# Mixer heads: tiles weighed in the turn of their argument, the pair's second head sum behind the weights' products

## The chip, the cores and the metric

The kernel runs on one core of one Trainium2 chip. The metric is the device time of one execution in microseconds (us). Engines are named as in the profile: PE (TensorE matmul), PEld (its weight loads), DVE (VectorE), ACT (ScalarE), POOL (GpSimd), SP (SyncE, which issues the DMAs).

## What is computed

The reference is two transformer blocks over 512 tokens of width 1024. The stage that matters here is in the first block's token mixer. It holds the four heads of an mLSTM (`M_HEADS` 4, head width 128), and beside them the preparation of eight RWKV-7 heads, in four pairs. The reference writes the mLSTM in chunks; what it computes per head is

```python
d = jnp.where(causal, b[..., :, None] - b[..., None, :] + logi[..., None, :], -jnp.inf)
p = jnp.exp(d - m_t[..., None]) * jnp.einsum('bhctd,bhcsd->bhcts', q, k)
num = ... + jnp.einsum('bhcts,bhcsv->bhctv', p, v)
den = ... + jnp.sum(p, -1)
h = num / jnp.maximum(jnp.abs(den), jnp.exp(-m_t))[..., None]
hm = standardize_heads(h, NORM_EPS)
y_m = jax.nn.sigmoid(o) * hm * m_norm_g
```

and, for the RWKV heads, what a pair's preparation makes of the projected rows:

```python
w = jnp.exp(-DECAY_SCALE * jax.nn.sigmoid(r_w0 + jnp.tanh(wd) @ r_w_up))
a = jax.nn.sigmoid(r_a0 + ad @ r_a_up)
kk = kk / jnp.maximum(jnp.sqrt(jnp.sum(kk * kk, -1, keepdims=True)), 1e-12)
kr = kr * (1.0 + (a - 1.0) * r_ka)
yr = yr + jnp.sum(rr * kr * r_rk, -1, keepdims=True) * vr
```

## The kernel before

All engines run programs of their own, tied by semaphores. Work is in stages; the change is in one of them, in the function `mlstm` (L1348). It computes a head over the whole sequence at once: for head h and block j of 128 keys, the scores against the queries from block j on, a tile of 128 keys by 512, 384, 256 or 128 queries. That makes sixteen **turns**, n = 4h + j, in a loop that each engine has in its own program. The order of the work in a turn is written out by hand.

What belongs to tile n, and the lines that show in the profile:

- DVE, `argument` (L1527): the exponent's argument from the row `top_b` and a column, two instructions, L1536 and L1537, into one of four buffers `m_e`. The buffer must be free of tile n-4.
- ACT: the exponent, L1685; right behind it the cast of a streamed weight tile to its high half (L388), on which POOL's subtraction for the low half depends (L397, `split_low`). I call POOL's part the split.
- PE: the scores, L1580, which wait until the tile before the last is weighed (the score banks are two).
- DVE, `weigh` (L1517): L1523 multiplies the scores in PSUM into the tile, L1525 multiplies its first 128 columns with the causal mask; both operands of L1525 are in SBUF. I call it the masking multiply.
- PE, `nums` (L1410): the weights' products, L1418 with the values and L1419 with ones, summed over the head's four tiles.

Beside them, in each turn:

- PE emits 4 + 4 steps of **fill**: the projection of another 128 columns of the first block, three fp32r products of 128x512 a step (L436, L437, L438). DVE (or ACT, for the four jobs "o") takes the finished job out of PSUM in the next turn; on DVE that is `shifted`, L1810 and L1812.
- The head before is normed: PE sums (`norm_sums`, L1474 in step j = 1, L1478 in j = 2), ACT (`norm_functions`, L1486, L1487, L1490, L1493), DVE (`norm_values`: L1499 centring in j = 1, L1504 and L1506 in j = 2, the reciprocal L1510 in j = 3) and `norm_end` (L1513, L1515) at the start of the next head.
- A pair of RWKV heads is prepared (`Operands`, L1816), step (n-1) % 4 in turn n, from turn 1 on. Step 0 (j = 1): PE's gate products, L1837 and at the end of the turn L1853; ACT's sigmoids L1860 and L1864; DVE L1889 to L1899. Step 1 (j = 2): PE's first head sum L1842, ACT's root L1870 and exponents, DVE L1903 and the reciprocal L1904. Step 2 (j = 3): DVE L1906, L1907 and the bonus terms L1909. Step 3 (j = 0 of the next head): PE's second head sum L1846, a product of `ones_half` with the bonus terms; DVE L1914, L1915, L1916 and, with that sum, L1921, which says that the pair's operands are made; POOL L1930 and L1932. L1837 of the next pair waits for L1921.
- Two rows per head are spread over the partitions by PE (`spread_top` at the end of turn 4h+3, `spread_low` at j = 0, both L1429, four rows of weights) and copied by ACT (L1460, L1467).

Before the change DVE weighs tile n-1 at the start of turn n, ahead of the argument of tile n:

```python
            for n in range(MH * ST):
                h, j = divmod(n, ST)
                if n:
                    weigh(dve, chain, n - 1)
                argument(dve, chain, n)
```

On PE the scores, the low row's spread and, in turns 4, 8 and 12, the second head sum stand ahead of the fill and the weights' products of tile n-1. Behind the loop comes the rest of the stage: the last head's norm, the last pair's step 3, the last fill job, and the recurrence's first group (L2006, L2021, L2163 and on), which goes on over the same engines.

Of the kernel before, what the change touches and what calls it, by code (L numbers as in the profile page):

```python
# [30 lines left out]
ST = S // P  # L31
# [6 lines left out]
MW, MH, MHD = 512, 4, 128  # L38
# [1309 lines left out]
def mlstm(k, h_in, arriving, early, qk, v, o, rkv, wa, gd, lora, lora_g, pairs, rooms, core, raw, norm):  # L1348
# [51 lines left out]
    fill = Fill(k, jobs, arriving, early=early)  # L1400
    GATES_JOB, WA, VALUES, UNITS = (2 * MH + i for i in range(4))
    arrived = lambda pair, part: fill.taken(names.index(f"{part}{pair.p}"))
# [3 lines left out]
    def prep(n):  # L1406

        return [(pairs[(n - 1) // ST], (n - 1) % ST)] if 0 < n <= MH * ST else []
# [35 lines left out]
    def spread_low(pe, h):  # L1444
        if h == 0:

            pe.wait_ge(*G("floor_ready").ge(2))
        if h < MH - 1:
            pe.wait_ge(*G("spread_taken").ge(top_nth(h + 1)))
        else:  # L1450

            pe.wait_ge(*G("var_ready").ge(h))
        spread(pe, low, h)
# [85 lines left out]
    with k.stage() as block:  # L1539
# [15 lines left out]
        @block.tensor  # L1555
        def _(pe):
            fill.pe(pe, 2 * DT + DT // 2)
            arriving.pe_sums(pe)
            fill.pe(pe, DT // 2)
            arriving.pe_turns(pe)  # L1560
            fill.pe(pe, (2 * MH + 2 + ST) * DT - 3 * DT)

            pe.wait_ge(*G("rows_ready").ge(1))
            for t in range(ST):
                last = nc.tensor.matmul(k.banks[SPREAD][:, t * MH:(t + 1) * MH], u[:, t * P:(t + 1) * P],
                                        k.const("ident", MH)[:, 0:MH], start=True, stop=True)
            last.then_inc(*G("turned_ready").inc())
            spread_top(pe, 0)
            fill.pe(pe, 4)

            pe.wait_ge(*fill.taken(VALUES))
            pe.wait_ge(*G("silu_ready").ge(2 * MH))
            pe.wait_ge(*k.tables_landed)
            pe.wait_ge(*k.lora_landed)
            for n in range(MH * ST):
                h, j = divmod(n, ST)
                if n >= 2:

                    pe.wait_ge(*prob.ge(n - 1))
                nc.tensor.matmul(k.banks[SCORE[n % 2]][:, 0:width[j]], qk[h][:, 1, j * P:(j + 1) * P],  # L1580
                                 qk[h][:, 0, j * P:S], start=True, stop=True).then_inc(*sent.inc())
                if h and j == 0:
                    spread_low(pe, h - 1)
                for pair, step in prep(n):
                    if step == 3:
                        pair.pe(pe, 2)
                fill.pe(pe, 4)
                if n:
                    nums(pe, n - 1)
                if h:  # L1590
                    norm_sums(pe, h - 1, j)
                for pair, step in prep(n):
                    if step < 2:
                        pair.pe(pe, step)
                if n:
                    fill.pe(pe, 4)
                for pair, step in prep(n):
                    pair.pe_late(pe, step)
                if j == ST - 1 and h + 1 < MH:
                    spread_top(pe, h + 1)  # L1600

            fill.pe(pe, 4)
            nums(pe, MH * ST - 1)
            fill.pe(pe, 4)
            spread_low(pe, MH - 1)

            pe.wait_ge(*G("operands_made").ge(2))
            pe.wait_ge(*G("values_made").ge(4))
            core.pe_turn(pe, 0, 0, range(2))
            pe.wait_ge(*fill.taken(LAST - 1))  # L1610
            core.pe_turn(pe, 0, 0, range(2, 3))

            pe.wait_ge(*G("den_ready").ge(MH))
            core.pe_turn(pe, 0, 0, range(3, 4))
            norm_sums(pe, MH - 1, 1)
            last_pair.pe(pe, 2)

            pe.wait_ge(*fill.taken(LAST))
            core.pe_products(pe, 0, 0)
            norm_sums(pe, MH - 1, 2)  # L1620
            core.pe_z(pe, 0, 0)

            core.pe_lane_free(pe, 0)
            pe.wait_ge(*G("var_ready").ge(MH))
            pe.wait_ge(*G("operands_made").ge(PAIRS))
            pe.wait_ge(*G("values_made").ge(2 * PAIRS))
            core.pe_turn(pe, 0, 1, range(4))
            core.pe_products(pe, 0, 1)
            core.pe_gate(pe, 0)
            core.pe_z(pe, 0, 1)  # L1630
            core.pe_gate(pe, 1)
            core.pe_rest(pe, 0)
            core.pe_group(pe, 1)
# [86 lines left out]
        @block.vector  # L1720
        def _(dve):
            chain = Chain(dve, G("dve_step"))
            nc.vector.memset(hm[:, 0:1], 0.0).then_inc(*G("gains_ready").inc())
            early.dve(dve, 0, 4)
            k.split_first(dve)
            early.dve(dve, 4, DT)
            arriving.dve_adds(dve, 0, 4)
            arriving.dve_adds(dve, 4)
            arriving.dve_roots(dve)

            dve.wait_ge(*arriving.named("turned_ready").ge(1))
            nc.vector.tensor_copy(hm[:], k.banks[arriving.turn_bank]).then_inc(*G("high_made").inc())
            arriving.dve_parts(dve, 0, DT)
            c = VECTORS["mu_rkv"]
            chain(nc.vector.tensor_scalar(k.keep_share[:], k.vecs[:, c:c + 15], -1.0, 1.0, ALU.mult, ALU.add))
            for t in range(2 * MH):
                fill.take(dve, chain, t)
            fill.take(dve, chain, GATES_JOB)
            dve.wait_ge(*G("gate_taken").ge(1))
            nc.vector.scalar_tensor_tensor(out=tmp, in0=fpre, scalar=-1.0, in1=fpre, op0=ALU.mult,  # L1740
                                           op1=ALU.max).then_inc(*G("abs_ready").inc())
            fill.take(dve, chain, WA)

            dve.wait_ge(*G("ln_ready").ge(1))
            chain(nc.vector.scalar_tensor_tensor(out=fpre, in0=fpre, scalar=0.0, in1=tmp, op0=ALU.min, op1=ALU.subtract))
            chain(nc.vector.tensor_tensor_scan(run, fpre, fpre, 0.0, ALU.add, ALU.bypass))
            nc.vector.tensor_tensor(u, ipre, run, ALU.subtract).then_inc(*G("rows_ready").inc())
            dve.wait_ge(*G("rows_ready").ge(1))
            chain(nc.vector.tensor_tensor_scan(top, u, u, 0.0, ALU.max, ALU.max))
            nc.vector.tensor_tensor(low, top, run, ALU.add).then_inc(*G("rows_ready").inc())  # L1750

            dve.wait_ge(*G("floor_ready").ge(1))
            chain(nc.vector.tensor_scalar(low, low, EPS, 1e-37, ALU.mult, ALU.max))
            nc.vector.tensor_scalar(low, low, 1e37, None, ALU.min).then_inc(*G("floor_ready").inc())

            dve.wait_ge(*G("turned_ready").ge(1))
            nc.vector.tensor_copy(u_col[:].rearrange("p t h -> p (t h)"), k.banks[SPREAD][:, 0:ST * MH]).then_inc(*G("turned_taken").inc())
            dve.wait_ge(*G("turned_taken").ge(1))
            dve.wait_ge(*k.tables_landed)
            for n in range(MH * ST):  # L1760
                h, j = divmod(n, ST)
                if n:
                    weigh(dve, chain, n - 1)
                argument(dve, chain, n)
                if h >= 2 and j == 0:
                    norm_end(dve, chain, h - 2)
                if n and jobs[UNITS + n - 1].engine == "dve":
                    fill.take(dve, chain, UNITS + n - 1)
                if n == MH * ST - 1:
                    weigh(dve, chain, n)  # L1770
                if h:
                    norm_values(dve, chain, h - 1, j)
                if n == MH * ST - 1:
                    norm_end(dve, chain, h - 1)
                for pair, step in prep(n):
                    pair.dve(dve, step, arrived)
            fill.take(dve, chain, LAST)
            norm_values(dve, chain, MH - 1, 1)
            last_pair.dve(dve, 3, arrived)
            core.dve_masks(dve, 0, 0, 0)  # L1780
            norm_values(dve, chain, MH - 1, 2)
            core.dve_masks(dve, 0, 0, 1)
            core.dve_masks(dve, 0, 0, 2)
            norm_values(dve, chain, MH - 1, 3)
            norm_end(dve, chain, MH - 1)
            for step in range(3):
                core.dve_masks(dve, 0, 1, step)
            core.dve_rest(dve, 0)
            core.dve_group(dve, 1)
# [2625 lines left out]
```

## Time and profile before

| | us |
|---|---|
| median of 3 runs | 1657.27 |
| lowest, highest | 1655.9, 1658.98 |
| profiled execution, its own time | 1661.74 |
| its span, first to last instruction | 1660.0 |
| PE busy in the span | 1594.6 (96%) |
| DVE busy in the span | 913.0 (55%) |
| mean granted clock of PE | 0.995 |

Times in rows of a timeline are us from the start of the span. The ends of products on PE are modelled, so starts are the better measure there. In windows the columns are the busy us (with the number of instructions) of PE, PEld, DVE, ACT and POOL, then the granted PE clock as a share of 2.4 GHz, the DMA share and GB/s. The stage's loop lasts from about 98 to 256 us.

### The profile page before, as it was taken

Reading aid. Unit: us, or ns where it says so; the run is one execution under the profiler, and the core shown is the slowest. Engines: PE = TensorE matmul, PEld = TensorE weight load, DVE = VectorE, ACT = ScalarE, POOL = GpSimd, SP = SyncE. Lnnn points to the kernel's source line nnn. Section 1 sums busy time; section 2 is a strip of 40 time slices with the busy share of each in tenths; the row PEclk is TensorE's granted clock in tenths of the full one; section 3 lists DMA queues with packets and bytes.
Section 4 is the critical chain, followed back from the end, with each engine's and each line's share of the span. In section 5 each row is a group of like instructions: output and inputs, shape, how many; then the busy total and the mean of one; then the engine's idle time right before and its main releaser. Section 6 shows DMA issues by size and latency. Waiting matters only on the chain. (4 is left out here: it accounts for less than half of the span.)

```text
span 1660.0 us, 25020 instructions
## 1 busy us (share of the span) xinstructions
PE 1594.6 (96%) x10298; PEld 1228.3 (74%) x10298; DVE 913.0 (55%) x1464; ACT 689.9 (42%) x1184; POOL 712.8 (43%) x357
## 2 busy tenths in 40 slices
PE   6999998889999899999999999999999999999999
PEld 5876666778787588888888888566576577787787
DVE  5957878545852336565541148597736663324251
ACT  4544444333432443222232334433645456355441
POOL 4533336244653144555554446264133422463342
PEclk9999999999999999999999999999999999999999
DMA  5421111003432032333233333112112310442132
GB/s 183 136 78 62 51 51 53 4 29 91 152 115 76 14 102 77 100 102 101 91 103 95 105 116 124 34 64 77 39 45 68 99 61 29 140 157 84 52 100 78
DMA packets 39713, 138.54 MB, mean 83 GB/s; under 512 B 4400, under 2 KB 5680, under 8 KB 38320
## 3 DMA queue, kind: packets, MB, share of 16 engines
q1 hardware_dynamic: 39600, 136.94, 25.8%
q8 instruction: 82, 1.34, 0.3%
q14 instruction: 31, 0.25, 0.0%
HBM read 132.73 MB, written 4.19 MB: 82 GB/s over the span
## 5 line engine op out<-in xcount | busy, mean ns | idle before, releaser
L397 POOL TENSOR_TENSOR parts<-ring,parts 128x1024 fp32r<-128x1024 f32 (+3 forms) x250 | 582.1, 2335 | 800.4 <-ACT parts L388 800.2
L436 PE MATMUL banks<-h_hi,parts 128*128 128x512 f32 x1120 | 462.6, 413 | 3.4 <-PEq L296 3.4
L438 PE MATMUL banks<-h_hi,parts 128*128 128x512 f32 x1120 | 437.3, 390 | 0.0
L437 PE MATMUL banks<-h_lo,parts 128*128 128x512 f32 x1120 | 436.9, 390 | 0.0
L388 ACT CAST parts<-ring 128x1024 fp32r<-128x1024 f32 (+3 forms) x251 | 244.7, 978 | 134.7 <-PE banks L438 134.6
L436 PEld LDWEIGHTS banks<-h_hi,parts 128*128 128x128 f32 x1120 | 211.0, 188 | 63.1 <-issue 19.6
L437 PEld LDWEIGHTS banks<-h_lo,parts 128*128 128x128 f32 x1120 | 211.0, 188 | 46.7 <-issue 6.1
L438 PEld LDWEIGHTS banks<-h_hi,parts 128*128 128x128 f32 x1120 | 210.5, 188 | 45.0
L3131 ACT CAST ffn_act_hi<-ffn_gate 128x512 fp32r<-128x512 f32 x22 | 13.7, 622 | 162.9 <-DVE ffn_gate L3030 162.9
L436 PE MATMUL banks<-ffn_act_hi,parts 128*128 128x512 f32 x176 | 68.5, 389 | 0.0
L437 PE MATMUL banks<-ffn_act_lo,parts 128*128 128x512 f32 x176 | 68.5, 389 | 0.0
L438 PE MATMUL banks<-ffn_act_hi,parts 128*128 128x512 f32 x176 | 68.5, 389 | 0.0
L3087 DVE TENSOR_TENSOR ffn_raw<-banks,ffn_root 128x512 f32<-128x512 f32 x22 | 15.2, 691 | 87.2 <-PE banks L438 87.1
L3097 DVE TENSOR_TENSOR x<-x,banks 128x512 f32<-128x512 f32 x8 | 5.5, 687 | 88.3 <-PE banks L438 88.3
L1075 DVE SCALAR_TENSOR_TENSOR ffn_gate<-ffn_raw,vecs,ffn_gate 128x511 f32<-128x511 f32 (+1 forms) x44 | 50.4, 1145 | 1.6
L2754 ACT ACTIVATE scores<-scores,row_stats 128x128 f32<-128x128 f32 (+3 forms) x64 | 35.5, 556 | 29.9 <-DVE row_stats L2732 29.8
L1071 DVE TENSOR_SCALAR ffn_gate<-ffn_raw,vecs 128x512 f32<-128x512 f32 x22 | 42.3, 1924 | 0.8
L436 PEld LDWEIGHTS banks<-ffn_act_hi,parts 128*128 128x128 f32 x176 | 33.0, 188 | 6.9
L437 PEld LDWEIGHTS banks<-ffn_act_lo,parts 128*128 128x128 f32 x176 | 33.0, 188 | 6.9
L438 PEld LDWEIGHTS banks<-ffn_act_hi,parts 128*128 128x128 f32 x176 | 33.0, 188 | 6.7
L2742 DVE TENSOR_SCALAR scores<-scores,row_stats 128x128 f32<-128x128 f32 (+3 forms) x64 | 34.6, 541 | 2.3
L2794 ACT ACTIVATE h_hi<-x,vecs 128x512 fp32r<-128x512 f32 x16 | 11.6, 726 | 50.9 <-DVE x L3076 27.1
(607 smaller groups left out, 2978.5 us busy)
## 6 DMA issues: line engine op xcount, KB each, us to landing
ring<-weights SPq DMA_DIRECT2D x211, 512.0 KB, 3.5
ring<-weights SPq DMA_DIRECT2D x24, 256.0 KB, 2.6
x<-xT SPq DMA_DIRECT2D x4, 1024.0 KB, 6.0
ring<-weights SPq DMA_DIRECT2D x8, 384.0 KB, 3.1
x_spill<-x SPq DMA_DIRECT2D x2, 1024.0 KB, 4.8
x<-x_spill SPq DMA_DIRECT2D x1, 2048.0 KB, 9.3
outT<-x SPq DMA_DIRECT2D x8, 256.0 KB, 2.0
ring<-weights SPq DMA_DIRECT2D x8, 192.0 KB, 2.4
```

The costliest lines, as they stand in the source:

```text
L388: self.nc.scalar.copy(self.parts[:, t % PARTS, 0, 0:w], self.ring[:, t % SLOTS, 0:w]).then_inc(self.high_ready, 1)
L397: self.nc.gpsimd.tensor_tensor(self.parts[:, t % PARTS, 1, 0:w], self.ring[:, t % SLOTS, 0:w], self.parts[:, t % PARTS, 0, 0:w].bitcast(F3 ...
L436: nc.tensor.matmul(out, w.hi, x.hi, start=first, stop=False)
L437: nc.tensor.matmul(out, w.hi, x.lo, start=False, stop=False)
L438: return nc.tensor.matmul(out, w.lo, x.hi, start=False, stop=last)
L1071: chain(nc.vector.tensor_scalar(dst, bank, k.vec(f"{weights}{taps - 1}", tile), k.vec(bias, tile), ALU.mult, ALU.add))
L1075: ins = nc.vector.scalar_tensor_tensor(out=dst[:, lag:S], in0=bank[:, 0:S - lag], scalar=k.vec(f"{weights}{j}", tile), in1=dst[:, lag:S], ...
L2742: nc.vector.tensor_scalar(scores(j - 1, e), scores(j - 1, e), st[:, 3:4], None, ALU.mult).then_inc(*scaled.inc())
L2754: nc.scalar.activation(scores(j, e), scores(j, e), ACT.Exp, bias=small[:, u % NS, 1:2], scale=-1.0, accum_out=small[:, u % NS, 2:3]).then_ ...
L2794: nc.scalar.mul(self.h.hi[:, m, :], k.x[:, m, :], k.vec(self.gain, m)).then_inc(*G("h_high").inc())
L3087: nc.vector.tensor_tensor(r, bank(gate_job(f)), root, ALU.mult).then_inc(*G("gate_taken").inc())
L3131: nc.scalar.copy(act_t.hi[:, f, :], gate[:, f % GATES, :]).then_inc(*G("act_high").inc())
```

## The change

In PE's turn, the fill's first four steps and the weights' products of tile n-1 now stand ahead of the second head sum (step 3 of a pair, turns 4, 8 and 12). In DVE's turn, tile n is weighed in turn n itself, behind its argument, the end of the norm two heads before and the take of a fill job; tile n-1 is no longer weighed at the start. In turns with j = 3, the pair's step (with the bonus terms) stands ahead of the norm's reciprocal; in the other turns the norm values come first, as before.

```diff
@@ PE, turn n
                 if h and j == 0:
                     spread_low(pe, h - 1)
+                fill.pe(pe, 4)
+                if n:
+                    nums(pe, n - 1)
                 for pair, step in prep(n):
                     if step == 3:
                         pair.pe(pe, 2)
-                fill.pe(pe, 4)
-                if n:
-                    nums(pe, n - 1)
                 if h:
                     norm_sums(pe, h - 1, j)
@@ DVE, turn n
                 h, j = divmod(n, ST)
-                if n:
-                    weigh(dve, chain, n - 1)
                 argument(dve, chain, n)
                 if h >= 2 and j == 0:
                     norm_end(dve, chain, h - 2)
                 if n and jobs[UNITS + n - 1].engine == "dve":
                     fill.take(dve, chain, UNITS + n - 1)
-                if n == MH * ST - 1:
-                    weigh(dve, chain, n)
-                if h:
+                weigh(dve, chain, n)
+                if h and j < ST - 1:
+                    norm_values(dve, chain, h - 1, j)
+                for pair, step in prep(n):
+                    pair.dve(dve, step, arrived)
+                if h and j == ST - 1:
                     norm_values(dve, chain, h - 1, j)
                 if n == MH * ST - 1:
                     norm_end(dve, chain, h - 1)
-                for pair, step in prep(n):
-                    pair.dve(dve, step, arrived)
             fill.take(dve, chain, LAST)
```

## Rows read from the trace of the kernel before

**Rows 1.** The page, part 1: busy us, share of the span, instructions

```profile
PE 1594.6 (96%) x10298; PEld 1228.3 (74%) x10298; DVE 913.0 (55%) x1464; ACT 689.9 (42%) x1184; POOL 712.8 (43%) x357
```

**Rows 2.** Windows of ten us: busy us by engine, granted clock, DMA

```profile
198.00:208.00 10.00, 9.63 (x40) 7.07 (x39) 8.61 (x12) 6.90 (x10) 3.36 (x2) 1.00 0.16 54
208.00:218.00 10.00, 9.65 (x27) 5.17 (x26) 9.76 (x13) 2.73 (x4) 3.77 (x2) 0.83 0.16 52
```

**Rows 3.** Waits in the stage, 90 to 270 us: total us, times, longest

```profile
DVE m_hm L1499 <- PE banks L1474: 14.5, 4, 6.0
...
PE banks L1418 <- DVE m_e L1525: 3.4, 8, 0.8
```

**Rows 4.** Timeline of PE, turns 2, 3: start us, us, what, [idle before]

```profile
117.43 0.39 PE L437 MATMUL banks<-h_lo,parts 128*128 128x512 f32 x1
117.66 0.39 PE L438 MATMUL banks<-h_hi,parts 128*128 128x512 f32 x1
118.41 0.91 PE L1418 MATMUL banks<-m_e,m_v 128*128 128x384 f32 x2 [0.37 <-DVE m_e L1525]
...
127.36 0.70 PE L1418 MATMUL banks<-m_e,m_v 128*128 128x256 f32 x2 [0.82 <-DVE m_e L1525]
```

**Rows 5.** Timeline of PE, turns 4, 8, 12: the head sum and its surroundings

```profile
134.40 2.07 PE L1846 MATMUL banks<-x,consts 128*128 128x512 f32 x2
...
139.65 0.38 PE L1418 MATMUL banks<-m_e,m_v 128*128 128x128 f32 x2
...
174.54 1.12 PE L1846 MATMUL banks<-x,consts 128*128 128x512 f32 x2 [0.38 <-DVE x L1909]
...
178.25 0.38 PE L1418 MATMUL banks<-m_e,m_v 128*128 128x128 f32 x2
...
213.12 2.08 PE L1846 MATMUL banks<-x,consts 128*128 128x512 f32 x2 [0.35 <-DVE x L1909]
...
218.31 0.38 PE L1418 MATMUL banks<-m_e,m_v 128*128 128x128 f32 x2
```

**Rows 6.** Timeline of POOL: two of the splits of weights

```profile
102.06 2.44 POOL L397 TENSOR_TENSOR parts<-ring,parts 128x1024 fp32r<-128x1024 f32 x1 [6.95 <-ACT parts L388]
...
198.37 2.85 POOL L397 TENSOR_TENSOR parts<-ring,parts 128x1024 fp32r<-128x1024 f32 x1 [9.66 <-ACT parts L388]
```

**Rows 7.** Tile m_e: the masking multiply, ns min/median/max

```profile
L1525 DVE TENSOR_TENSOR m_e<-m_e,consts x16: 291/291/2274, 102.6 to 247.9; 128x128 f32<-128x128 f32 x16
```

**Rows 8.** Timeline of DVE: turns 0, 10 to 13, the stage end

```profile
102.61 2.04 DVE L1525 TENSOR_TENSOR m_e<-m_e,consts 128x128 f32<-128x128 f32 x1
...
195.43 0.56 DVE L1523 SCALAR_TENSOR_TENSOR m_e<-banks,m_e 128x384 f32<-128x384 f32 x1
...
196.23 0.35 DVE L1536 TENSOR_SCALAR m_e<-top_b,u_col 128x256 f32<-128x256 f32 x1
...
198.27 0.68 DVE L1504 TENSOR_TENSOR y<-y,floor_b 128x512 f32<-128x512 f32 x1
...
204.92 0.42 DVE L1523 SCALAR_TENSOR_TENSOR m_e<-banks,m_e 128x256 f32<-128x256 f32 x1
...
217.21 1.38 DVE L1914 COPY decay<-x 128x8 f32<-128x8 f32 x1
...
219.10 1.78 DVE L1916 TENSOR_TENSOR rkv<-x,rkv 128x512 f32<-128x512 f32 x1
220.92 0.69 DVE L1921 TENSOR_TENSOR rkv<-banks,rkv 128x512 f32<-128x512 f32 x1
...
259.86 0.69 DVE L1499 SCALAR_TENSOR_TENSOR m_hm<-banks,m_hm 128x512 f32<-128x512 f32 x1 [1.25 <-PE banks L1474]
```

**Rows 9.** Timeline of PE: the gate products of a pair

```profile
187.50 1.12 PE L1837 MATMUL banks<-wa,lora_wa 64*128 64x512 f32 x2
...
191.50 1.12 PE L1853 MATMUL banks<-wa,lora_wa 64*128 64x512 f32 x2
...
231.56 1.12 PE L1853 MATMUL banks<-wa,lora_wa 64*128 64x512 f32 x2
```

## The prediction

> **What bounds the kernel now.** I read the page first: PE is busy for 96% of the span [rows 1], so only what makes PE wait or slows it is worth time. The change touches one stage, the sixteen turns from about 98 to 256 us. Its windows of ten us show PE busy for 9.6 us or more of each ten, DVE for up to 9.8 [rows 2]. So the gain can only be the rest of PE's time and its clock, and DVE is the engine that could take PE's place. I then took the waits of the stage, and the timelines of PE, DVE, ACT and POOL through it.
>
> PE loses time in three ways. First, the weights' products (L1418) wait for DVE's masking multiply (L1525): eight times, 3.4 us by the column of idle time [rows 3]. The starts tell more, since idle time is counted from a modelled end. A fill product starts 0.23 us after the one before; the first of these waits starts 0.75 us after, so 0.52 us are lost; the one with 0.82 us of idle time lost 0.97 [rows 4]. The other six (turns 6, 7, 10, 11, 14, 15) look like the first. They are alike because DVE is itself tied to PE: it masks the tile as the last thing after work that waited for PE's gate product or head sum.
>
> Second, the pair's second head sum (L1846) waits for DVE's bonus terms (L1909) in turns 8 and 12, 0.38 and 0.35 us [rows 5]; turn 4 shows none.
>
> Third, the clock. From the start of L1846 to the weights' products of the same turn stands the same work each time: 3.71 us in turn 8, but 5.25 in turn 4 and 5.19 in turn 12 [rows 5]. The window of turn 12 has a granted clock of 0.83 [rows 2], a mean over 2.4 GHz and a stretch at 1.2. Ahead of each such place PE runs four full-width f32 products in a row with L1846 the last, two of them with four rows of weights. The falls cost 1.48 and 1.54 us.
>
> **The change part by part.** No instruction is added or removed, no DMA moves, SP and POOL keep their orders; what changes is PE's order within a turn and DVE's.
>
> Weighing in the turn of the argument: DVE now weighs tile n a turn sooner, ahead of the norm values and the pair's step. PE wants tile n only in the middle of its turn n+1. In turn 10 the tile would be ready some 5 us after DVE's argument, and PE asks for it a turn later. All eight waits go: 7 x 0.52 + 0.97 = 4.6 us. The price on DVE is a wait for ACT's exponent and PE's score. Where a fill tile is taken between the two (1.5 us), the exponent is done before. Where ACT takes the fill (turns 5, 9, 13), DVE waits some 0.6 us for it; queued behind is the centring L1499, which waits for PE anyway, 14.5 us in four times [rows 3]. So nothing.
>
> The head sum behind the products, its terms ahead of the reciprocal: the terms no longer stand behind DVE's reciprocal of the head, and they are wanted 3.3 us later (twelve fill products of 0.23 and two narrow pairs). The 0.38 and 0.35 go, with their ends some 0.8 us. On DVE the bonus product L1921 waits for this sum, and the next turn's argument is queued behind it. In turn 12 PE would end the sum at 213.12 + 3.3 + 0.9, less what it gained, so before 217.3, while DVE stands at L1921 at 220.92 [rows 5, 8]. Nothing.
>
> The clock: between the spread of the row and the head sum now stand twelve fill products, so the row of f32 products ends a quarter sooner. Both falls go, 3.0 us; the other end is that neither goes. I take that they go: turn 8 shows that even the long row of f32 products does not always lower the clock, and the window of turn 10, with pairs of them between fills, is at 1.00 [rows 2].
>
> Sum of what PE gains: 4.6 + 0.8 + 3.0 = 8.4 us.
>
> Against it stands a price on DVE. POOL splits a weight tile each turn, started by ACT's cast, which follows ACT's exponent: 2.44 us long when alone [rows 6]. The masking multiply takes 0.29 us, but 2.04 us in turn 0, where it begins within such a split and ends with it; before, this was seldom, the median being 0.29 [rows 6 to 8]. In the new order it is the rule. In turn 10 the argument starts at 196.23, the split at 198.37, 2.14 later; the take ends at 198.27, and behind a weighing of 0.42 the masking multiply would start 2.5 us after the argument and stand until the split ends at 4.6 [rows 6, 8]. That is 2.1 us of delay in turns of this kind, and as much in turns 11 and 14; in turn 12, 0.5. The Trainium skill (SBUF — State Buffer, Who interferes with whom) says that a DVE instruction with two SBUF inputs and a POOL instruction exclude each other and the first holds the port to its end; by that rule, too, DVE pays here and POOL does not, and the trace agrees in turn 0.
>
> What it costs PE is read on the loop from one pair's second gate product (L1853) to the next pair's, since DVE hangs on the first and PE's L1837 on DVE's L1921. PE's own loop is 231.56 - 191.50 = 40.06, less 0.52, 0.52, 0.4 and the fall of 1.48: 37.1 us [rows 9]. DVE's: L1921 ends at 221.61, 30.1 after L1853; add two delays of 2.1; in turn 12 the waits of 1.2 and 1.1 that L1914 and L1916 have behind POOL now (1.38 and 1.78 us for some 0.2 and 0.7 of work [rows 8]) give way to 0.5 and about 1.2, so less 0.6; and 4.0 from L1837 to L1853 [rows 9]: 37.7. PE waits 0.6 us at L1837 in turns 9 and 13: 1.2 us. The bounds: 0 if the splits miss, 1.8 each if POOL goes ahead at each meeting.
>
> At the end of the stage DVE is late by the delay of turn 14 (2.1) and does not share PE's last two gains (1.05), but has the 0.8 us of one weighing moved out of its way and 1.25 us of slack ahead of L1499 [rows 8]: 1.1, call it 1.0 us late. The recurrence behind it hangs on DVE, so this counts. Turns 2 and 3, with the same collisions, come ahead of the first head's norm work, where DVE has time to spare; nothing.
>
> 8.4 - 1.2 - 1.0 = 6.2 us. The stages behind are chains relative to this one, and weights are far ahead there, so I take the shift to reach the end. The span goes from 1660.0 to 1653.8. The profiled execution took 1661.74, so 1655.5 in its like. It is 4.5 us over the median, so the runs may have fewer falls of the clock; I leave the sum as it is: 1657.27 - 6.2 = 1651.1.
>
> **Rivals.** (A) The forecast, gain 3.8 (PE waits 1.8 us at L1837 in both turns, for 0.6) to 7.4 (no wait there), so 1649.9 to 1653.5.
>
> (B) The collisions cost PE nothing: split and multiply miss each other, or slack covers it. Gain 8.4, 1648.9 us. For it: in turn 10 the multiply would begin only 0.4 us after the split. Against: turn 11's narrow tile is weighed well inside the split.
>
> (C) The falls of the clock stay, as the three f32 products ahead remain: 8.4 - 3.0 - 2.2 = 3.2 us gained, 1654.1. For it: in turn 4 the clock fell with PE never idle, and in turn 8 it held in the same order, so the row alone does not decide. The Trainium skill (TensorE: Matmul & The Clock Gate, What's actually happening) has the clock go down after idleness and stay up under work; by that rule the order of products would change nothing, as in this rival; turn 4 speaks against the rule.
>
> (D) Slower: DVE becomes the bound. Place: DVE from the argument of turn 10 to L1921 in turn 12, and its like one head before. If POOL's products each go ahead (1.2 and 1.1) and each split is itself stretched to the 2.85 us of [rows 6], the loop is 37.7 + 2.3 + 0.8 = 40.8, and PE waits 3.7 at L1837 twice; with 1.4 at the end and a fall of 1.5 behind each wait: 8.4 - 7.4 - 1.4 - 3.0 = -3.4, 1660.7 us. It decides from a loop over 39.3 us, the mean of the two as they are.
>
> (E) It does not do what it says for the end: PE's time is won in the stage and lost behind it, in the recurrence or by other falls of the clock. Within 0.2%, near 1656.
>
> **How the numbers follow.** A 0.50, B 0.15, C 0.19, D 0.06, E 0.10. Likeliest is A, 1651.1. The range takes A, B but for its edge, and C with some of E: 1648.3 to 1655.5. A measurement of this kernel can tell about 0.2%, 3.3 us, from no change. C lies on that line and goes half and half: faster 0.75, same 0.19, slower 0.06.
>
> **What would show it.** In the changed profile: L1418 waits for L1525 nowhere, L1846 for L1909 nowhere; the time from the head sum on shows no clock of 0.83; the median of L1525 goes from 0.29 to near 2 us (B: it does not); PE waits at L1837 in turns 9 and 13 for L1921, 0 to 1.8 us; L1499 of the stage's end starts 6 us sooner. I am wrong if the stage ends sooner but the kernel does not, if the masking multiply stays short, or if the clock falls in the same places.

## The result, and the profile after

The changed kernel is slower: 1663.72 us, the median of 22 runs (1660.04 to 1667.86), against 1658.98 for before in 21 runs beside it. The ratio is 1.0026, with a 95% interval of 1.0017 to 1.0035. Medians, means and ratios here and below leave out four executions of over 2000 us: one of before beside this kernel, one of before and two of e8 later. I had forecast 1651.1 with a range up to 1655.5, and 0.06 for a slower kernel. The profiled execution took 1660.88 us, among the shortest of its kind, where that of before (1661.74) was among the longer ones; so the two spans, 1659.1 and 1660.0, stand the wrong way round, and I compare them place by place.

The waits of PE in the stage (98 to 262 us) of the changed kernel: total us, times, longest.

```profile
PE banks L2005 <- ACT y L1487: 3.9, 1, 3.9
PE banks L436 <- DVE rkv L1811: 3.4, 3, 1.6
```

The same view of before: 

```profile
PE banks L1418 <- DVE m_e L1525: 3.4, 8, 0.8
PE banks L1846 <- DVE x L1909: 0.7, 2, 0.4
PE banks L2006 <- ACT y L1487: 0.2, 1, 0.2
```

The waits that were to go have gone, all ten. In their place PE's fill (L436) waits three times for DVE's take of a fill tile, and the first product of the recurrence (L2005, the L2006 of before) waits 3.9 us for ACT in place of 0.2. Rows name lines by their own kernel's numbers, which differ by up to three from those of before behind the changed part: the terms L1906 to L1909 of before are L1905 to L1908 here.

The masking multiply (tile m_e, L1525, ns min/median/max) is long nearly always, as forecast; before, the median was 291 [rows 7]:

```profile
L1525 DVE TENSOR_TENSOR m_e<-m_e,consts x16: 291/2197/2250, 101.1 to 243.0; 128x128 f32<-128x128 f32 x16
```

The windows of ten us (columns as in [rows 2]) show the head sum's window at clock 1.00, where it was 0.83 [rows 2], but PE busy for 8.41 us in place of 9.65; and the stage's end, where before had 10.00 busy in 248 to 258 us:

```profile
208.00:218.00 10.00, 8.41 (x36) 6.20 (x35) 9.82 (x11) 2.55 (x4) 3.61 (x2) 1.00 0.10 34
248.00:258.00 10.00, 6.05 (x26) 3.36 (x25) 8.12 (x8) 2.64 (x5) 1.37 (x2) 0.92 0.17 53
258.00:268.00 10.00, 7.26 (x201) 5.17 (x200) 8.57 (x15) 6.41 (x9) 7.51 (x5) 0.84 0.32 109
```

Measured by the starts of PE's scores (L1580), the lead over before grows from 1.5 us at the loop's start (a fall of the clock near 24 us, in the profile of before alone) to 7.1 us in turn 15: 5.6 us won in the loop, the two falls of the clock among them. From one turn's scores to the next, a turn that had one of the waits for L1525 is 0.63 to 0.64 us shorter now, turn 3 with the long one 1.08; the turns 9 and 13, in which the fill waits for the take, are 1.31 and 1.83 longer. At PE's last spread (L1429) the lead is 6.6 us, at the last group of the recurrence's first products (L2006, here L2005) 2.9, and at L1499 2.5 (257.39 against 259.86 [rows 8]). The place where it goes is seen in DVE's timeline of turn 15:

```profile
242.97 2.25 DVE L1525 TENSOR_TENSOR m_e<-m_e,consts 128x128 f32<-128x128 f32 x1
245.14 0.68 DVE L1905 TENSOR_TENSOR x<-x 128x512 f32<-128x512 f32 x1
245.85 2.79 DVE L1906 TENSOR_TENSOR qk<-qk,x 128x512 f32<-128x512 f32 x1
248.68 0.75 DVE L1908 SCALAR_TENSOR_TENSOR x<-rkv,vecs,x 128x512 f32<-128x512 f32 x1
249.35 3.35 DVE L1510 RECIPROCAL y<-y 128x512 f32<-128x512 f32 x1
252.73 0.75 DVE L1513 SCALAR_TENSOR_TENSOR m_hm<-m_hm,vecs,y 128x512 f32<-128x512 f32 x1
253.52 0.69 DVE L1515 TENSOR_TENSOR y<-m_hm,m_o 128x512 f32<-128x512 f32 x1
```

The pair's terms (L1905 to L1908) now stand ahead of the reciprocal and the norm's end, and two of the seven instructions run into POOL's splits at 242.65 and 245.50. The first of these, 2.25 us, is not new: the masking multiply of this turn took 2.27 us before too. New are L1906 with 2.79 us and the place of the terms. So L1515 starts only 0.83 us sooner than before, where PE is 6.6 ahead. Before:

```profile
254.35 0.69 DVE L1515 TENSOR_TENSOR y<-m_hm,m_o 128x512 f32<-128x512 f32 x1
```

In the changed kernel L1515 ends at 254.2, and ACT and PE hang on it one behind the other:

```profile
254.30 0.58 ACT L1486 COPY m_hm<-banks 128x512 f32<-128x512 f32 x1 [3.65 <-DVE y L1515]
```

```profile
255.44 0.66 PE L2005 MATMUL banks<-consts,rkv 128*128 128x128 f32 x4 [3.95 <-ACT y L1487]
```

Later a second loss stands in the state steps of the recurrence, at 375 to 385 us, 2.4 us large. The second of PE's steps (L2399, here L2398) starts 4.08 us behind the first, where it was 2.60. The experiments come back to it.

### The profile page after: what moved, and what is told of

It reads as the page before. It is cut to its first block and busy times, and to the rows that moved or that the text cites. A ratio compares the mean times of both kernels' runs of the same rounds, so it can differ in the third digit from the quotient of the medians.

```text
span 1659.1 us, 25026 instructions
## 1 busy us (share of the span) xinstructions
PE 1593.0 (96%) x10298; PEld 1228.8 (74%) x10298; DVE 930.3 (56%) x1464; ACT 689.8 (42%) x1184; POOL 707.5 (43%) x357
## 5 line engine op out<-in xcount | busy, mean ns | idle before, releaser
L436 PE MATMUL banks<-h_hi,parts 128*128 128x512 f32 x1120 | 461.4, 412 | 6.8 <-DVE rkv L1811 3.4
L436 PEld LDWEIGHTS banks<-h_hi,parts 128*128 128x128 f32 x1120 | 210.5, 188 | 69.3 <-issue 21.3
L436 PE MATMUL banks<-ffn_act_hi,parts 128*128 128x512 f32 x176 | 68.5, 389 | 0.0
L436 PEld LDWEIGHTS banks<-ffn_act_hi,parts 128*128 128x128 f32 x176 | 33.0, 188 | 6.9
```

What stands on the lines that cost most here:

```text
L436: nc.tensor.matmul(out, w.hi, x.hi, start=first, stop=False)
```

## The experiments

Times scatter mainly with the clock: over all runs of the study 0.001 less mean granted clock goes with 1.3 us. Beside each median and ratio I therefore give the difference of the means at an equal clock of 0.995, by that slope; its standard error is 0.3 to 0.5 us. Where an edit itself makes PE idle and its clock fall, as in e2, this difference leaves part of the loss out. The experiments were timed in three groups, each with before again: 1659.55 us in 29 runs for e1 to e4, 1660.90 in 34 for e5 to e8, 1658.65 in 29 for e9 to e11; ratios and differences are against the group's own. The clocks of before's runs beside the changed kernel are not on record, so its difference is taken against the first group's: +4.0 us (+3.5 against the second's, +5.1 against the third's). Where an experiment is compared with the changed kernel, that spread stands behind it.

In the experiments D names the theory that the loss sits on DVE (not the prediction's rival D), P that PE's new order costs, L that the last turn alone does it; F, that the place of DVE's instructions in its stream matters.

**PE's move alone** (e1_pe_only): DVE as before.

```
                 fill.pe(pe, 4)
                 if n:
                     nums(pe, n - 1)
+                for pair, step in prep(n):
+                    if step == 3:
+                        pair.pe(pe, 2)
```

> Only PE's part of the change: the second head sum (L1846) stands behind the fill's first four steps and the weights' products; DVE is as before. Theory D (the loss sits on DVE: the masking multiply stands behind POOL's split, DVE is late at the stage's end, PE waits for ACT's L1486 and its clock falls): 0 to 2 us faster than before (the L1846 waits of 0.8 us go, and the falls of the clock in turns 4, 8 and 12 where a run has them). Theory P (PE's new order costs): 2 to 4 us slower. In the profile by both: L1525 keeps a median of 0.29 us and L1418 waits for it eight times.

1658.02 us in 11 runs against 1659.55 for before in 29; ratio 0.9986 (0.9973 to 0.9998); at equal clock -1.35, as D had it. P is out. The waits for L1909 are gone, the eight for L1525 are there as before:

```profile
PE banks L1418 <- DVE m_e L1525: 3.3, 8, 0.8
```

**DVE's weighing alone** (e2_weigh_only): `weigh(dve, chain, n)` behind the take, with the second head sum and the pair's step where they were.

> Only the weighing in the turn of the argument; PE's order and the place of the pair's step behind the norm values are as before. Theory D: the masking multiply has a median of 2.2 us, and the stage's end is late by the collisions of turns 14 and 15: 1 to 3 us slower than before. Theory L (what costs is the last turn alone, the end of the norm of head 2 behind the pair's step, on which ACT's L1486 waits): 2 to 5 us faster than before, since the last turn keeps its order here. PE waits for L1846's terms up to 2 us in turns 8 and 12 by both.

1669.9 us in 6 runs, ratio 1.0062 (1.0048 to 1.0076); at equal clock +5.5. PE's head sum, still ahead of the fill, now waits for bonus terms that stand behind the weighing and the reciprocal:

```profile
PE banks L1843 <- DVE x L1906: 9.9, 2, 5.0
```

Both theories expected waits of up to 2 us there, and the run is 10 us slower by the medians, beyond D's 3: the clock, 0.9917 in the mean against 0.9951, fell behind the waits. The weighing needs one of the other two parts, and L as the only cause is out.

**The mask on the scores** (e3_mask_in_psum): the changed kernel, the mask multiplied into the scores in PSUM, ahead of the weighing.

```
+        chain(nc.vector.tensor_tensor(score[:, 0:P], score[:, 0:P], k.const("key_le_query"), ALU.mult))
         nc.vector.scalar_tensor_tensor(out=ed, in0=score[:, 0:width[j]], ...
-        nc.vector.tensor_tensor(e[:, n % 4, 0:P], e[:, n % 4, 0:P], k.const("key_le_query"), ALU.mult)
```

> The changed kernel with the mask multiplied into the scores in PSUM, ahead of the weighing, so that the masking multiply has one operand in SBUF instead of two; same count of instructions. Theory D: the multiply is short (about 0.3 us) though POOL's split runs beside it, the wait of PE for ACT's L1487 at the stage's end shrinks from 4 us to under 2, and the kernel is 3 to 6 us faster than the changed one, about as fast as before or 1 to 2 us faster. Theory L: the multiply is short, but PE still waits 2 us or more at the end: at most 2 us faster than the changed kernel. Theory P: no more than 1 us off the changed kernel.

1664.11 us in 12 runs, ratio 1.0024 (1.0015 to 1.0034); at equal clock +2.4. By the ratio that is no faster than the changed kernel, against D's expectation of 3 to 6 us and within L's; at equal clock 1.6 us may be won, the fill's waits for the take are 2.1 us in place of 3.4, and the state steps lose less in this profile (below). The bulk stays, 3.7 us of waiting at the stage's end among it: the masking multiply is short now, but the next instruction with two inputs in SBUF has its wait. DVE in turn 15 of this kernel:

```profile
242.59 0.29 DVE L1524 TENSOR_TENSOR banks<-banks,consts 128x128 f32<-128x128 f32 x1
242.92 0.29 DVE L1525 SCALAR_TENSOR_TENSOR m_e<-banks,m_e 128x128 f32<-128x128 f32 x1
243.13 2.43 DVE L1906 TENSOR_TENSOR x<-x 128x512 f32<-128x512 f32 x1
245.59 2.81 DVE L1907 TENSOR_TENSOR qk<-qk,x 128x512 f32<-128x512 f32 x1
```

So the collision belongs to the split's time and not to the masking multiply: whatever of the kind follows the take pays the rest of the split.

**The last turn in before's order** (e4_last_turn): in turn 15 the reciprocal, `norm_values` and `norm_end` stand ahead of the pair's step.

```
-                if h and j < ST - 1:
+                last = n == MH * ST - 1
+                if h and (j < ST - 1 or last):
                     norm_values(dve, chain, h - 1, j)
+                if last:
+                    norm_end(dve, chain, h - 1)
```

> The changed kernel with the order of before in the last turn alone: the reciprocal and the end of the norm of head 2 ahead of the pair's step. Theory D: PE's wait at the stage's end shrinks from 4 us by the pair's step (2.1 us, and 2.1 more where its L1907 stood behind a split), so 2 to 4 us faster than the changed kernel, still no faster than before by more than 1 us. Theory L: 4 us or more faster than the changed kernel, and 1 us or more faster than before. Theory P: within 1 us of the changed kernel.

1660.74 us in 12 runs, ratio 1.0003 (0.999 to 1.0016); at equal clock +0.4, so 3.6 less than the changed kernel, as D had it; L had expected a kernel faster than before. The wait at the stage's end is 0.2 us again, the window of 248 to 258 us has PE busy for 9.17:

```profile
PE banks L436 <- DVE rkv L1812: 3.5, 3, 1.7
PE banks L1478 <- issue: 0.9, 1, 0.9
PE banks L2006 <- ACT y L1487: 0.2, 1, 0.2
```

**The state steps.** In the changed kernel, e2 and e4, all with the new weighing, PE's second state step stands 4.1 us behind the first; before and in e1 it is 2.6. In e3 it is 2.63: there a stretch at half clock (376 to 380 us at 0.57) brought the first step late, and DVE's add met only the end of POOL's split (0.94 us); the fourth step is 1.0 us late. The new order makes the kernel six instructions longer, with DVE's arithmetic the same in number: the pages count 25026 against 25020, and x1464 for DVE in both. I put them down to wait instructions in DVE's stream. To see whether that is all, e5_before_waits takes before and adds only waits that are long satisfied, and e6_last_turn_waits moves the stream of e4 on by two:

```
             dve.wait_ge(*k.tables_landed)
+            for _ in range(13):
+                dve.wait_ge(*k.tables_landed)
             for n in range(MH * ST):
```

> Before, with 13 waits more on DVE ahead of the mlstm loop, on a load that has long landed: six instructions more in DVE's stream, as the changed kernel has, and no other difference. F (the 2.4 us at the state steps come from where DVE's instructions stand: the first add L2405 starts some 0.46 us behind its satisfied wait in place of 0.10, so L2407 loses the port to POOL's split): the second state step starts 4.1 us behind the first in place of 2.6, and the run is slower than before by 1.5 to 2.8 us. W (the loss comes from the weighing's order by some state that it leaves behind, such as POOL's or ACT's lead): the distance stays 2.6 and the time is before's within 0.5 us.

1663.42 us in 12 runs against 1660.90 for before in 34; ratio 1.0017 (1.0003 to 1.0032); at equal clock +2.8. DVE at the first state step, before:

```profile
380.26 0.43 DVE L2405 TENSOR_TENSOR state<-banks,decay 128x256 f32<-128x256 f32 x1 [1.40 <-PE banks L2399]
380.72 0.42 DVE L2407 TENSOR_TENSOR state<-state,gain 128x256 f32<-128x256 f32 x1
```

and with the waits (its lines are higher by one):

```profile
377.63 0.42 DVE L2406 TENSOR_TENSOR state<-banks,decay 128x256 f32<-128x256 f32 x1 [1.76 <-PE banks L2400]
378.09 2.37 DVE L2408 TENSOR_TENSOR state<-state,gain 128x256 f32<-128x256 f32 x1
```

```profile
377.77 4.96 POOL L397 TENSOR_TENSOR parts<-ring,parts 128x1024 fp32r<-128x1024 f32 x2 [16.48 <-ACT parts L388]
```

```profile
380.51 0.68 PE L2400 MATMUL banks<-state,step_T 64*64 64x64 f32 x16 [1.41 <-DVE state L2408]
```

The multiply from the bank starts 0.36 us later behind the same product. The add behind it has two inputs in SBUF; before, it started 0.05 us ahead of POOL's split, at 380.72 against 380.77, and took 0.42; here the split begins at 377.77, 0.32 us ahead of the add, which takes 2.37. The second step starts 1.5 us late by this and the fourth, behind another such meeting, 2.4 (10.2 us behind the first in place of 7.8). F holds, with no other edit in the kernel.

> The last-turn variant (label e4_last_turn) with 5 such waits, two instructions more in DVE's stream, so that the late instruction is another one than L2405. F: the second state step starts 2.6 us behind the first, the run is faster than e4_last_turn by 1.5 to 2.8 us, so about 1658.3, level with before. W: distance 4.1, time as e4_last_turn within 0.5 us.

1658.47 us in 11 runs, ratio 0.998 (0.9969 to 0.9992); at equal clock -1.7. The second step stands 2.59 us behind the first, and against e4 2.1 us are won, as F had it. This version is faster than before and than the changed kernel.

> The changed kernel with 5 redundant waits on DVE ahead of the loop (two instructions more in its stream), and nothing else. F: the second state step starts 2.6 us behind the first in place of 4.1, and of the loss against before 2 to 3 us are gone: ratio 1.0005 to 1.0015. G (e6 gained against e4 by something else, the time of the runs being scattered by the clock): ratio 1.002 or above.

The changed kernel with five such waits: 1660.98 us in 11 runs against 1658.65 for before in 29; ratio 1.0015 (1.0006 to 1.0025); at equal clock +2.5. F's distance is there, its time only at the edge: 1.5 us of the changed kernel's +4.0 are gone, not 2 to 3, and the interval reaches into G. The second step stands 2.6 us behind the first:

```profile
380.30 0.42 DVE L2405 TENSOR_TENSOR state<-banks,decay 128x256 f32<-128x256 f32 x1 [1.41 <-PE banks L2399]
380.76 0.43 DVE L2407 TENSOR_TENSOR state<-state,gain 128x256 f32<-128x256 f32 x1
```

> Before with 17 such waits, eight instructions more in DVE's stream in place of e5_before_waits' six. F (place decides, not number): the second state step starts 2.6 us behind the first, the time is before's within 0.7 us. H (the waits' number costs, each a little, or any shift of the stream from before's does it): distance 4.1, slower than before by 1.5 us or more.

Before with eight instructions more: 1660.25 us in 12 runs, ratio 1.0011 (1.0 to 1.0023); at equal clock +0.5. The distance is 2.59, so the place in the stream and not the number of waits makes the loss at the state steps. The time itself misses F's 0.7 us and would suit H: 1.6 us over before's median, of which the clock of these runs (0.9947 against 0.9956) goes with 1.1. Whether the rest is a price of the waits stays open.

All thirteen profiles agree on the place. With 25020 instructions (before, e1, e8) or 25028 (e6, e7, e9, e10, e11) DVE's multiply starts 0.82 or 0.83 us behind the start of the first state step; with 25026 (the changed kernel, e2, e3, e4, e5) it starts 1.18 to 1.20 us behind.

**The take ahead of the norm's end** (e7_take_ahead): e6 with these two exchanged.

```
                 argument(dve, chain, n)
+                if n and jobs[UNITS + n - 1].engine == "dve":
+                    fill.take(dve, chain, UNITS + n - 1)
                 if h >= 2 and j == 0:
                     norm_end(dve, chain, h - 2)
-                if n and jobs[UNITS + n - 1].engine == "dve":
-                    fill.take(dve, chain, UNITS + n - 1)
```

> e6_last_turn_waits with the fill's take ahead of norm_end in turns 8 and 12. T (the three waits of the fill L436 for the take L1812, 1.0, 1.6 and 0.8 us, are PE time lost and come from the 1.4 us of L1513 and L1515 ahead of the take): two of them go, 1.5 to 2.6 us faster than e6_last_turn_waits, so about 1656, faster than before by 2 to 3.5 us. N (the bank would be waited for by another, or POOL's next split comes into the take's place): within 0.7 us of e6_last_turn_waits.

1661.0 us in 11 runs, ratio 0.9998 (0.9984 to 1.0011); at equal clock +0.3, so 2.0 slower than e6. Both theories missed in the time; N had its words, that the wait goes elsewhere. The waits of L436 went from 3.4 to 1.1 us, but:

```profile
PE banks L1418 <- DVE m_e L1525: 3.4, 2, 1.8
PE banks L436 <- DVE rkv L1813: 1.1, 2, 0.8
```

DVE in turn 8 shows why. POOL's split starts at 177.25, some 2.6 us behind the argument as in e6; L1515 stood ahead of it there and stands behind its start here, and the weighing stands behind L1515:

```profile
176.27 0.75 DVE L1813 SCALAR_TENSOR_TENSOR rkv<-banks,vecs,rkv 128x511 f32<-128x511 f32 x1
176.94 0.74 DVE L1513 SCALAR_TENSOR_TENSOR m_hm<-m_hm,vecs,y 128x512 f32<-128x512 f32 x1
177.71 2.81 DVE L1515 TENSOR_TENSOR y<-m_hm,m_o 128x512 f32<-128x512 f32 x1
```

**The reciprocal first in every turn** (e10_recip_first): e6 with `if h: norm_values(...)` ahead of the pair's step in turns 7 and 11 too.

> e6_last_turn_waits with the reciprocal of the head sums ahead of the pair's step in turns 7 and 11 too, as before the change. R (the terms ahead of the reciprocal are what lets PE's second head sum run without a wait): PE waits at L1845's product for the bonus terms in two turns, 0.5 to 3 us each, and the run is slower than e6_last_turn_waits by 1 to 5 us. S (PE's move behind the weights' products gives the terms time enough): no such wait, the time within 0.7 us of e6_last_turn_waits.

1655.83 us in 12 runs against 1658.65; ratio 0.9987 (0.9975 to 0.9999); at equal clock -1.6, as e6. R's waits are there and S's time is:

```profile
PE banks L1845 <- DVE x L1908: 3.2, 2, 1.7
PE banks L1478 <- issue: 0.5, 1, 0.5
PE banks L436 <- DVE rkv L1811: 0.2, 1, 0.2
```

3.2 us of waits at the head sum replace 3.2 of the 3.4 at the takes. So in these two kernels the order of DVE's work only chooses where PE waits for it. That DVE has this much too much to do between one pair and the next is my reading; no run took work off it.

**PE's move and the terms, without the weighing** (e8_pe_and_terms).

> Before with PE's move and with the pair's step ahead of the reciprocal save in the last turn; the weighing stays as before. D (what was lost is owed to the weighing's place in the last turn and to the instructions it adds, and the rest of the change is sound): as e1_pe_only within 1 us, 1657 to 1658.5, faster than before. Q (the terms ahead of the reciprocal hold back norm_values for the banks L1515 waits for, and cost by themselves): slower than e1_pe_only by over 1 us.

1664.11 us in 10 runs against 1660.90; ratio 1.0015 (1.0002 to 1.0027); at equal clock +2.2, and 3.6 slower than e1 by that measure. Q holds for the time, by another wait than it named:

```profile
PE banks L1418 <- DVE m_e L1525: 5.9, 10, 1.3
```

The two new waits stand in turns 9 and 13 (1.28 and 1.25 us). They begin in turns 7 and 11. In e1 the reciprocal follows the take in turn 7; it runs beside a split that starts at 169.09 and keeps its length:

```profile
169.10 3.34 DVE L1510 RECIPROCAL y<-y 128x512 f32<-128x512 f32 x1
```

In e8 the terms follow the take, and L1910 (the L1907 of before), with two inputs in SBUF, meets the split that starts at 168.76:

```profile
169.48 2.79 DVE L1910 TENSOR_TENSOR qk<-qk,x 128x512 f32<-128x512 f32 x1
```

That makes DVE 2.1 us late, and PE feels it at the tiles of turns 8 and 12:

```profile
186.04 1.12 PE L1418 MATMUL banks<-m_e,m_v 128*128 128x512 f32 x2 [1.28 <-DVE m_e L1525]
```

So D's view that the rest of the change is sound piece by piece is wrong: the terms ahead of the reciprocal need the new weighing, whose masking multiply takes the collision in turns 7 and 11 (L1906 took 0.69 us there in the changed kernel).

**The clock, over all profiles.** No run was made for the clock, but the thirteen profiles tell of it. All three kernels with the order of before on PE and DVE (before, e5, e11) show the clock fall in turn 4 and in turn 12, and none between 256 and 280 us. With PE's move and the old weighing (e1, e8) the fall of turn 12 is gone and that of turn 4 stays. With the new weighing turn 4 has none even where PE's order is the old one (e2), and the changed kernel, e3, e4, e6, e7, e9 and e10 have neither. The windows of 130 to 140 and 208 to 218 us, first of e5, then of e1:

```profile
130.00:140.00 10.00, 10.00 (x31) 5.98 (x30) 9.79 (x14) 3.72 (x6) 5.53 (x4) 0.83 0.29 88
208.00:218.00 10.00, 9.65 (x28) 5.42 (x29) 9.76 (x14) 3.24 (x6) 3.77 (x3) 0.83 0.19 54
130.00:140.00 10.00, 10.00 (x32) 6.01 (x30) 9.77 (x11) 3.03 (x5) 5.52 (x3) 0.83 0.16 54
208.00:218.00 10.00, 10.00 (x37) 6.01 (x36) 9.76 (x13) 3.83 (x6) 3.77 (x2) 1.00 0.16 52
```

But of the ten kernels in which a fall had gone, nine have one between 256 and 280 us (all but e7), just behind the stage. There is one profile of each kernel, so that this fall comes of the edits is likely and not shown. Before, and then the changed kernel:

```profile
256.00:276.00 20.00, 16.46 (x420) 11.58 (x420) 18.20 (x26) 11.60 (x19) 10.06 (x7) 1.00 0.19 71
256.00:276.00 20.00, 17.26 (x411) 12.10 (x410) 17.08 (x24) 9.69 (x15) 10.41 (x8) 0.83 0.16 56
```

## Why the prediction was wrong

In the order of its own sum:

- **Eight waits of L1418, 4.6 us: right** as such; none is left. By the scores' starts they were worth a little more, 7 x 0.63 + 1.08 = 5.5 us, turn 15 taken like the others. **The 0.8 us of L1846: right**; e1 shows the waits gone with PE's move alone, and turn 8 is 0.40 us shorter in the changed kernel.
- **The collisions: right in kind.** The median of L1525 is 2197 ns, behind the take, as the arithmetic of turn 10 had it. The Trainium skill (SBUF — State Buffer, Who interferes with whom) has the pair excluding each other; e3 and e7 agree and add that a removed collision moves to the next instruction of that kind (2.43 and 2.81 us).
- **"PE waits 0.6 us at L1837 in turns 9 and 13: 1.2 us": wrong in place and size; the first step that failed.** PE waits there not at all. I priced DVE's delay over the loop from L1853 to L1921 and did not ask which work on that loop PE wants first. It is the take: in turn 8 of the changed kernel DVE comes out of two collisions and two reciprocals and reaches the take at 175.2, and the fill of turn 9 waits for its bank. The measured price is 3.4 us of idle time in three waits, not 1.2 in two; by the starts it is 1.3 + 1.8 + 1.1 = 4.2 us, the third in turn 15.

```profile
176.79 0.50 PE L436 MATMUL banks<-h_hi,parts 128*128 128x512 f32 x1 [1.02 <-DVE rkv L1811]
215.60 0.50 PE L436 MATMUL banks<-h_hi,parts 128*128 128x512 f32 x1 [1.59 <-DVE rkv L1811]
```

- **"At the end of the stage ... call it 1.0 us late": the second, and the largest in the stage.** I followed the chain through L1499 alone. ACT's L1486 and L1487 wait for L1515, PE's first product of the recurrence for them, and there PE lost 3.7 us more than before (3.95 against 0.21). The part of the change that puts the terms ahead of the reciprocal does this in turn 15; I had costed it for the turns with a head sum behind it and not for the last one. e4 takes it back: 3.6 us.
- **"Both falls go, 3.0 us": the third.** They went, and as the profiles together show, this was the order of work and not chance: the fall of turn 12 went with PE's move, that of turn 4 with the new weighing, which the row of f32 products, my reason, does not explain. What failed is that the 3.0 us would be kept. Another fall stands behind the stage in nine of the ten kernels (here 256 to 260 us at 0.57, behind the wait of 3.95 us, and 264 to 272 at 0.83 and 0.74), and over the runs the mean clock is 0.9952, against 0.9951 for before in the first group: nothing is left of the term in the time. Rival C, with no gain there, had the better number for this term by the wrong reason, for it had the falls stay in place. The rule of the Trainium skill that I weighed there (TensorE: Matmul & The Clock Gate, What's actually happening) would have had me leave the 3.0 out, as the time does; with its reason the profiles do not agree, since the clock falls where PE was not idle, as in turn 4 before [rows 5], and the order of the work moved it.
- **"I take the shift to reach the end": the fourth.** 2.4 us went in a stage that the change does not touch, because the stream grew by six instructions (e5). I wrote that no instruction is added; of arithmetic that is so, of the kernel's 25020 instructions not. That L2407 won its race against the split by only 0.05 us stood in the trace of before, and I had not looked there.

Put together by the starts: 5.5 + 0.8 - 4.2 - 3.7 - 2.4 = -4.0 us, with the clock at nothing, against +4.0 measured at equal clock (+3.5 to +5.1, by the runs of before that are taken) and +4.3 by the ratio (0.0026 of 1658.98). That the two agree so closely is luck; the signs and the order of the terms are not. e6, without the last two terms, is faster than before by 1.7 at equal clock, where 5.5 + 0.8 - 4.2 gives 2.1.

Of the rivals D had the sign and its first words, that DVE becomes the bound; its place, L1837, was wrong, and so was its condition. A loop over 39.3 us was not needed, since the take and L1515 are due earlier than L1921. E had its mechanism in both its parts, a gain lost behind the stage in the recurrence and by other falls of the clock, but not its size: it stood at 1656.

## What to carry to other kernels

When work is added to or moved within a nearly full engine, list everything that others take from it in the same loop with its slack, and price the delay at the one due first; a loop's length alone names the wrong place. Do so again for the last turn, where other engines hang on other things. Look also in the stages behind for races that are won by less than 0.1 us: there six instructions more cost over half of the +4.0 us here, and padding the old kernel with satisfied waits showed it in one run. Before a fall of the clock is priced as a gain, look where the clock falls in every profile at hand: here it could be moved out of a turn, and the mean clock of the runs stayed.

## What the runs showed of the hardware

A satisfied wait costs little itself: eight instructions more went with +0.5 us at equal clock (e11). But six instructions more in DVE's stream made one instruction start 0.36 us late at the state steps (e5), and eight did not; in all thirteen profiles it is late with 25026 instructions and on time with 25020 and 25028. That the place in the stream decides is shown; why, no view here shows.

DVE and POOL took turns by whole instructions where DVE's had two inputs in SBUF, and who started first won: 0.05 us ahead, and the state add took 0.42 us; 0.32 behind, and it took 2.37. The reciprocal, with one input, kept its 3.34 us beside a split (e1). But in e3 a multiply of one SBUF tile by a column of scalars, L1889, stood 2.12 us where it met a split:

```profile
107.05 2.12 DVE L1889 TENSOR_SCALAR x<-rkv,vecs 128x512 f32<-128x512 f32 x1
```

PE's clock fell with PE at work: PE was busy for 10.00 of the 10 us in 130 to 140 us in before, e1, e5 and e11, each time at 0.83. The places recur: turns 4 and 12 with the order of before, 20 to 28 us in eight of the thirteen profiles. Where PE idled long it fell too: in e2 the window of 172 to 176 us, behind a wait of 5.0 us, is at 0.50:

```profile
172.00:176.00 4.00, 3.06 (x5) 1.84 (x6) 3.86 (x8) 1.56 (x2) 0.59 (x1) 0.50 0.00 0
```
